# Gate and up of a SwiGLU by seven block products (Strassen) in place of eight, on one core

## The chip, the cores and the metric

The kernel runs on one core of one Trainium2 chip. The metric is device time in microseconds (us), from one launch to its end. The program is one block of straight code and loops for each engine: TensorE (PE), VectorE (DVE), ScalarE (ACT), GpSimd (POOL), and the SyncE queue (SP), which issues every DMA. Engines order each other by semaphores only.

## The reference, cut to what matters

A one-layer encoder over 1024 prompt tokens and 32 sample tokens, all in float32. D_MODEL is 1024, D_FF is 2816.

```python
def swiglu(h, w_gate, w_up, w_down):
    return (jax.nn.silu(h @ w_gate) * (h @ w_up)) @ w_down

def reference(...):
    hp = rms_norm(yp, g_mix)
    q, k, v, u, g = project(hp, w_in)                  # 1792 columns
    a = window_attention_prompt(q, k, v, attn_sinks)
    m = gmlp_prompt(u, g, ...)
    yp = yp + concatenate([a, m]) @ w_out              # 1024 x 1024
    ...                                                # the same for ys
    yp = yp + swiglu(rms_norm(yp, g_ffn), w_gate, w_up, w_down)
    ys = ys + swiglu(rms_norm(ys, g_ffn), w_gate, w_up, w_down)
    y_prompt, y_sample = rms_norm(yp, g_final), rms_norm(ys, g_final)
```

## The kernel before, in words

Tokens are kept as 9 rows: eight tiles of 128 prompt tokens and one of the 32 sample tokens (`SAMPLE`), together `TOK` = 1056 columns. Every large product is made in three passes over fp32r operands (`three_passes`, L611): each operand x is split into a high part (an fp32r copy, by ACT) and a low part (x minus the high part, `low`, by DVE at L1058), and the passes are high*high, high*low and low*high, summed in PSUM. So each 128x128 weight tile of a product costs three pairs of weight load and matmul (L615, L616, L617).

The first part (norm, input projection, attention, gMLP) follows a list written out by hand, `SCHEDULE`. The projection works on 3 token blocks of 352 columns. The output projection follows, row by row (`out_proj`, L797): 48 matmuls of 512 columns for a row of 128 tokens, 32 for the sample row, with w_out in `wbuf`. DVE adds each row's two PSUM banks onto the residual (`add_out_proj`, L1259); ACT squares it, POOL forms the root, DVE scales it (`norm_front`), PE transposes it (`norm_back`, L649), and ACT and DVE write its high and low parts to `t_hl`. The residual of all nine rows stays in on-chip memory (`y_slots`).

The FFN is a loop over 11 chunks of 256 FFN columns (`chunk`, L868). In a chunk PE makes six gate-up steps (`gate_up`, L828: two tiles of 128 FFN columns, three blocks of 352 tokens), each of gate and up with 8 weight tiles and 3 passes, so 48 matmuls of 352 columns. ACT applies Silu, DVE multiplies, and ACT and DVE split the product into `act_hl`. Then PE makes the down product of that chunk for the nine rows (`down`, L850: 12 matmuls of 512 columns for a row of 128 tokens, 8 for the sample row), and DVE adds each row onto the residual (`add_down`, L1311), so the sum over all FFN columns is built up on chip, chunk by chunk. Weights come through a ring of three 4 KB stage slots, and ACT and DVE split them one chunk ahead. After the last chunk the rows are normed and stored.

## Time and profile before

| what | value |
|---|---|
| median of 3 runs | 1141.89 us (1140.77 to 1142.42) |
| profiled execution, its span from first to last instruction | 1140.8 us |
| PE busy | 1109.0 us, 97% of the span |
| PE weight loads busy | 1019.8 us, 89% |
| DVE busy | 482.5 us, 42% |
| ACT busy | 259.4 us, 23% |
| POOL busy | 32.8 us, 3% |
| moved by DMA | 62.71 MB, mean 55 GB/s |
| mean granted TensorE clock | 0.991 |

The span of the profiled execution is the lowest of the three times to 0.1 us, so no time of note lies outside it, and it lies 1.1 us under the median. Durations of matmuls overlap, because they are pipelined: the distance from one start to the next is what a matmul costs, not its length.

### The profile page before, as it was taken

To read this page: it belongs to the slowest core of one execution; us is meant where nothing else is said; L and a number is where in the kernel's file an instruction comes from. 1 tells how busy PE (TensorE), PEld (TensorE's weight loads), DVE (VectorE), ACT (ScalarE), POOL (GpSimd) and SP (SyncE) were. 2 spreads that over 40 slices of the span, in tenths; PEclk is the share of its full clock that TensorE was granted. 3 is DMA by queue.
4 is the path that set the end of the run, shared out by engine and by line. 5 is a ranking of instruction groups with operands and counts; after the bars stand their busy time and mean duration, and the time that the engine had idled before them with its cause. 6 is when DMAs were issued, how large, how long until landed. Compare 5 with 4: busy or idle time off the path is not lost.

```text
span 1140.8 us, 16333 instructions
## 1 busy us (share of the span) xinstructions
PE 1109.0 (97%) x6764; PEld 1019.8 (89%) x6764; DVE 482.5 (42%) x738; ACT 259.4 (23%) x525; POOL 32.8 (3%) x73
## 2 busy tenths in 40 slices
PE   5799999999999999999999999999999999999996
PEld 4799998888888989989899898999989999898995
DVE  4366547655334243342433424243252432524327
ACT  4321245434122211201112021120211211021123
POOL 2101100000000000000000000000000000000002
PEclk9899999999999999999999999999999999999998
DMA  8121332005010131112111021111111201112003
GB/s 279 45 59 39 76 78 57 20 21 189 1 36 3 37 93 31 44 37 55 55 37 53 20 55 55 37 55 37 45 47 37 73 19 55 37 37 74 19 1 153
DMA packets 76120, 62.71 MB, mean 55 GB/s; under 512 B 11888, under 2 KB 68272, under 8 KB 76080
## 3 DMA queue, kind: packets, MB, share of 16 engines
q1 hardware_dynamic: 76080, 62.15, 18.8%
q8 instruction: 29, 0.48, 0.2%
q14 instruction: 11, 0.09, 0.0%
HBM read 57.58 MB, written 4.65 MB: 55 GB/s over the span
## 4 chain that ended last, share of the span: by engine, by line
PE 96%; DVE 2%; ACT 1%; issue 0%; DMA 0%; POOL 0%; POOLq 0%; SPq 0%; ACTq 0%
PE ps L615 30%; PE ps L617 29%; PE ps L616 29%; PE ps L649 1%; PE ps L632 1%; PE ps L633 1%; PE ps L784 1%; DVE work L1078 1%; PE ps L762 1%; PE ps L714 1%; PE ps L746 1%; DMA gain<-in_g_mix 0%; PE ps L703 0%; PE ps L740 0%; ACT work L906 0%
## 5 line engine op out<-in xcount | busy, mean ns | idle before, releaser
L615 PE MATMUL ps<-t_hl,wbuf 128*128 128x352 f32 x864 | 286.1, 331 | 8.4 <-DVE t_hl L1058 8.4
L616 PE MATMUL ps<-t_hl,wbuf 128*128 128x352 f32 x864 | 280.2, 324 | 0.0
L617 PE MATMUL ps<-t_hl,wbuf 128*128 128x352 f32 x864 | 279.9, 324 | 0.0
L1251 DVE TENSOR_TENSOR work<-ps,work 128x1024 f32<-128x1024 f32 (+1 forms) x108 | 132.1, 1223 | 143.0 <-PE ps L617 142.5
L615 PEld LDWEIGHTS ps<-t_hl,wbuf 128*128 128x128 f32 x864 | 164.8, 191 | 10.9 <-DVE t_hl L1058 6.0
L615 PE MATMUL ps<-t_hl,gate_up_a 128*128 128x352 f32 x528 | 170.5, 323 | 0.0
L1298 DVE TENSOR_TENSOR trans<-ps,trans 128x352 f32<-128x352 f32 x66 | 34.6, 524 | 319.2 <-ACT trans L1020 319.2
L616 PE MATMUL ps<-t_hl,gate_up_a 128*128 128x352 f32 x528 | 169.2, 321 | 0.0
L617 PE MATMUL ps<-t_hl,gate_up_a 128*128 128x352 f32 x528 | 169.0, 320 | 0.0
L616 PEld LDWEIGHTS ps<-t_hl,wbuf 128*128 128x128 f32 x864 | 165.2, 191 | 0.0
L617 PEld LDWEIGHTS ps<-t_hl,wbuf 128*128 128x128 f32 x864 | 164.7, 191 | 0.0
L1020 ACT ACTIVATE trans<-ps 128x352 f32<-128x352 f32 x66 | 30.6, 464 | 568.5 <-PE ps L617 568.5
L615 PE MATMUL ps<-wbuf 128*128 128x512 f32 x352 | 138.7, 394 | 0.0
L617 PE MATMUL ps<-wbuf 128*128 128x512 f32 x352 | 138.4, 393 | 0.0
L616 PE MATMUL ps<-wbuf 128*128 128x512 f32 x352 | 137.7, 391 | 0.0
L1058 DVE TENSOR_TENSOR wbuf<-stage,wbuf 128x1024 fp32r<-128x1024 f32 x66 | 80.7, 1223 | 48.1 <-ACT wbuf L925 29.4
L615 PEld LDWEIGHTS ps<-t_hl,gate_up_a 128*128 128x128 f32 x528 | 99.0, 188 | 1.0
L616 PEld LDWEIGHTS ps<-t_hl,gate_up_a 128*128 128x128 f32 x528 | 99.2, 188 | 0.4
L617 PEld LDWEIGHTS ps<-t_hl,gate_up_a 128*128 128x128 f32 x528 | 98.9, 187 | 0.0
L617 PEld LDWEIGHTS ps<-wbuf 128*128 128x128 f32 x352 | 66.1, 188 | 15.4
L616 PEld LDWEIGHTS ps<-wbuf 128*128 128x128 f32 x352 | 66.4, 189 | 14.6
L615 PEld LDWEIGHTS ps<-wbuf 128*128 128x128 f32 x352 | 66.1, 188 | 14.0
(119 smaller groups left out, 997.2 us busy)
## 6 DMA issues: line engine op xcount, KB each, us to landing
stage<-in_w_gate SPq DMA_DIRECT2D x44, 256.0 KB, 3.1
stage<-in_w_up SPq DMA_DIRECT2D x44, 256.0 KB, 3.2
stage<-in_w_down SPq DMA_DIRECT2D x44, 256.0 KB, 3.6
work<-in_x_prompt SPq DMA_DIRECT2D x16, 512.0 KB, 6.5
stage<-in_w_in SPq DMA_DIRECT2D x28, 256.0 KB, 3.5
stage<-in_w_out SPq DMA_DIRECT2D x16, 256.0 KB, 3.8
out_y_prompt<-work SPq DMA_DIRECT2D x8, 512.0 KB, 2.6
gain<-in_g_mix SPq DMA_DIRECT2D x1, 512.0 KB, 5.4
```

The costliest lines, as they stand in the source:

```text
L615: mm(out, wh, xh, start=first, stop=False)
L616: mm(out, wh, xl, start=False, stop=False)
L617: return mm(out, wl, xh, start=False, stop=last)
L632: mm(out, x_both, w_hi, start=first, stop=False)
L633: t = mm(out, x_both, w_lo, start=False, stop=last)
L649: t = turn(out[:, k, 0:n], xn[rows, i % 2, P * k:P * k + P], ident[rows, rows])
L714: t = mm(out[:, P * x:P * x + n], vn[0:n, g % 2, i, :], wsp_t[0:n, g, 0:n], start=True, stop=True)
L746: last = mm(out[DH:P, at:at + P], cat[hp, j, odd:odd + DH], k_t[hp, even:even + P], start=True, stop=True)
L1020: nc.scalar.activation(silu[:, s % 2, :], ps[:, gate_bank(s), 0:BLK], ACT.Silu).then_inc(silu_ready, 1)
L1058: return nc.vector.tensor_tensor(out, x, hi.bitcast(F32), ALU.subtract)
L1251: nc.vector.tensor_tensor(y_row(i), banks(row_parts(i), b), y_row(i), ALU.add).then_inc(added, 1)
L1298: nc.vector.tensor_tensor(hidden[:, s % 2, :], ps[:, gate_bank(s) + 1, 0:BLK], silu[:, s % 2, :], ALU.mult).then_inc(hidden_ready, 1)
```

## The change

Gate and up of one tile of 128 FFN columns are one matrix product of a 2x2 block matrix of weights by a 2x2 block matrix of tokens. The weight blocks are A11 and A12 (gate, first and second half of the 1024 input dimensions) and A21 and A22 (up, likewise). The token blocks are B11 and B21 (rows with even number, first and second half of the dimensions) and B12 and B22 (rows with odd number). Eight block products are replaced by seven (Strassen, in Winograd's form): with sums S1 to S4 of weight blocks and T1 to T4 of token blocks. Each operand form is split in a high and a low part as before, so a block product is 4 tiles by 3 passes, 12 matmuls.

- A step is one tile of 128 FFN columns; there are 22. Each step goes over two halves of the tokens, 256 and 272 columns wide (row pairs 0/1, 2/3; row pairs 4/5, 6/7 and the two halves of the sample row), and makes the seven products in each.
- The seven token forms are made once, row by row, beside the output projection, by copies on ACT and subtractions on DVE. They fill most of on-chip memory. So the residual goes out to device memory (`y_scratch`) row by row after the output projection, and the rows of silu(gate)*up go there too (`hid_scratch`).
- The weight sums are made by four POOL operations of 128x512 in each step; ACT and DVE split all seven weight forms (seven copies and seven subtractions of 128x512).
- ACT copies P1, and P5 and P7 together, out of PSUM; P2, P3 and P4 are summed onto banks in PSUM; DVE makes the remaining sums.
- The down product comes after all 22 steps, with the same 11 chunks of 9 rows and the same matmuls. The chunks' hidden rows and weights are loaded by one DMA each, the residual is loaded back to on-chip memory, and `down` rotates over three pairs of banks in place of two.
- The projection's token blocks are 384, 384 and 288 columns wide, in place of three of 352.

```diff
+PRODUCTS = 7
+P1, P6, P5, P7, P2, P3, P4 = range(PRODUCTS)
+HALF_W = [256, 272]
+BANK_1, BANK_6, BANK_A, BANK_B = [2, 4], [3, 5], [0, 6], [1, 7]
...
             sp.wait_ge(cat_lo, ROWS)
+            load_y(0)
+            load_y(1)
+            for i in range(ROWS):
+                if i == SAMPLE:
+                    sp.wait_ge(wout_unit_done, 1)
+                    load_gate_up(0, 0)
+                    sp.wait_ge(wout_unit_done, 3)
+                    load_gate_up(1, 1)
+                sp.wait_ge(y_added, i + 1)
+                sp.dma_start(y_scratch[row_tokens(i), :], y_row(i)).then_inc(y_spilled[i % 2], 16)
+                if i + 2 < ROWS:
+                    load_y(i + 2)
...
+            def ffn_step(s, q, more):            # SP
+                if more:
+                    sp.wait_ge(w_form_lo, PRODUCTS * s + PRODUCTS)
+                    load_gate_up(s + 2, q)
+                for j in range(2):
+                    store_hidden(s, j)
...
+            last = STEPS - 1
+            sp.wait_ge(product_done, product_count(last, P1, 1))
+            for j in range(2):
+                sp.wait_ge(hidden_out[j], 16 * (STEPS - 2))
+            load_down(0, 0)
+            ffn_step(last - 1, 0, False)
+            sp.wait_ge(w_form_lo, PRODUCTS * STEPS)
+            for i in range(2):
+                sp.wait_ge(y_spilled[i], 16 * len(range(i, ROWS, 2)))
+            for i in range(6):
+                sp.dma_start(y_acc_row(i), y_scratch[row_tokens(i), :]).then_inc(y_back[i], 16)
+            sp.wait_ge(product_done, product_count(last, P3, 1))
+            for i in range(6, ROWS):
+                sp.dma_start(y_acc_row(i), y_scratch[row_tokens(i), :]).then_inc(y_back[i], 16)
+            sp.wait_ge(product_done, product_count(last, P4, 1))
+            load_down(1, 1)
+            ffn_step(last, 1, False)
+            for j in range(2):
+                sp.wait_ge(hidden_out[j], 16 * STEPS)
+            for c in range(2, CHUNKS):
+                load_down(c, c % 2)
...
+            def weight_sums(c, q):               # POOL
+                nc.gpsimd.tensor_tensor(s1, a21, a22, ALU.add).then_inc(w_sum_1, 1)
+                pool.wait_ge(w_sum_1, s + 1)
+                nc.gpsimd.tensor_tensor(s2, s1, a11, ALU.subtract).then_inc(w_sums_ready, 1)
+                nc.gpsimd.tensor_tensor(s3, a11, a21, ALU.subtract).then_inc(w_sums_ready, 1)
+                pool.wait_ge(w_sums_ready, 3 * s + 1)
+                nc.gpsimd.tensor_tensor(s4, a12, s2, ALU.subtract).then_inc(w_sums_ready, 1)
...
+            def product(s, p, j):                # PE
+                elif first and p == P5 and j == 0:
+                    pe.wait_ge(y_added, ROWS)
+                elif not first and p == P1:
+                    pe.wait_ge(c11_silu, 2 * s + (j - 1))
+                elif not first and p == P6:
+                    pe.wait_ge(u2_ready, 2 * s + (j - 1))
+                elif not first and p == P5:
+                    pe.wait_ge(c12_ready, 2 * s + (j - 1))
+                if p == P2:
+                    pe.wait_ge(p1_copied, 2 * s + (j + 1))
+                if p == P3:
+                    pe.wait_ge(p57_copied, 2 * s + (j + 1))
+                if j == 0:
+                    pe.wait_ge(w_form_lo, PRODUCTS * s + (p + 1))
+                for k in range(KH):
+                    w = [wf[:, p, h, k, :] for h in range(2)]
+                    x = [xf[j][:, X_OF[p], h, k, :] for h in range(2)]
+                    t = three_passes(ps[:, bank, 0:HALF_W[j]], w, x, opens and k == 0, k == KH - 1,
+                                     onto=not opens)
...
             for i in range(ROWS):                # ACT, beside the output projection
+                if i >= 1:
+                    plain_forms(i - 1)
+                if i == SAMPLE:
+                    weight_hi(0, 0, 0)
+                norm_front(ROWS + i)
+                if i >= 1:
+                    keep_blocks(i - 1)
...
+            def ffn_step(c, q):                  # ACT
+                copy_p1(s, 0)
+                copy_p57(s, 0)
+                silu_c11(s, 0)
+                silu_c12(s, 0)
+                copy_p1(s, 1)
+                for n in (0, 1, 2):
+                    weight_hi(*following, n)
+                copy_p57(s, 1)
+                weight_hi(*following, 3)
+                silu_c11(s, 1)
+                weight_hi(*following, 4)
+                weight_hi(*following, 5)
+                silu_c12(s, 1)
+                weight_hi(*following, 6)
...
             for i in range(ROWS):                # DVE, beside the output projection
+                if i == SAMPLE:
+                    weight_lo(0, 0, 0)
+                add_out_proj(i)
+                if i >= 1:
+                    if i % 2 == 1:
+                        even_low(i - 1)
+                    else:
+                        odd_blocks(i - 1)
+                if i == SAMPLE:
+                    weight_lo(0, 0, 1)
+                norm_front(ROWS + i)
+                if i >= 2 and i % 2 == 0:
+                    fourth_sum(i // 2 - 1)
+                    if i == SAMPLE:
+                        weight_lo(0, 0, 2)
+                        weight_lo(0, 0, 3)
+                    low_12(i // 2 - 1)
...
+            def blocks(s, j):                    # DVE
+                dve.wait_ge(product_done, product_count(s, P4, j))
+                dve.wait_ge(u2_ready, 2 * s + (j + 1))
+                if not isinstance(s, int) or s >= 1:
+                    dve.wait_ge(hidden_out[j], 16 * s)
...
+            p5_p7(last, 1)                       # DVE, the last step's second half
+            down_weight_lo(0)
+            act_lo(0)
+            blocks(last, 1)
+            hidden(last, 1)
+            for c in range(CHUNKS):
                 for i in range(ROWS):
                     add_down(c, i)
+                    if c + 1 < CHUNKS and i == 1:
+                        down_weight_lo(c + 1)
+                    if c + 1 < CHUNKS and i == 3:
+                        act_lo(c + 1)
```

## Rows read from the trace of the kernel before

**Rows 1.** The page: busy time by engine, and the chain by engine.

```profile
PE 1109.0 (97%) x6764; PEld 1019.8 (89%) x6764; DVE 482.5 (42%) x738; ACT 259.4 (23%) x525; POOL 32.8 (3%) x73
...
PE 96%; DVE 2%; ACT 1%; issue 0%; DMA 0%; POOL 0%; POOLq 0%; SPq 0%; ACTq 0%
```

**Rows 2.** Waits of PE: us in total, times, longest.

```profile
PE ps L649 <- DVE work L1078: 11.9, 4, 8.0
PE ps L615 <- DVE t_hl L1058: 8.4, 3, 4.7
```

**Rows 3.** Stretches of one FFN chunk each: length, busy by engine, clock, DMA.

```profile
371.80:441.50 69.70, 69.70 (x392) 64.86 (x393) 25.93 (x29) 11.51 (x19) 0.00 (x0) 1.00 0.19 53
441.50:511.50 70.00, 70.00 (x396) 65.15 (x395) 25.67 (x28) 11.71 (x19) 0.00 (x0) 1.00 0.17 45
```

**Rows 4.** Timeline of DVE: the sample row's add before and after the FFN.

```profile
362.71 1.22 DVE L1255 TENSOR_TENSOR work<-ps,work 32x1024 f32<-32x1024 f32 x1 [3.00 <-PE ps L633]
...
1132.29 1.22 DVE L1255 TENSOR_TENSOR work<-ps,work 32x1024 f32<-32x1024 f32 x1
```

**Rows 5.** Timeline of PE: first and last of 21 matmuls of 352 columns.

```profile
599.68 0.32 PE L615 MATMUL ps<-t_hl,wbuf 128*128 128x352 f32 x1
...
602.86 0.32 PE L617 MATMUL ps<-t_hl,wbuf 128*128 128x352 f32 x1
```

**Rows 6.** The same, first and last of 18 matmuls of 512 columns.

```profile
429.81 0.39 PE L617 MATMUL ps<-wbuf 128*128 128x512 f32 x1
...
433.72 0.39 PE L633 MATMUL ps<-wbuf 128*64 128x512 f32 x1
```

**Rows 7.** gMLP's mix, plain float32: matmuls and weight loads, merged.

```profile
87.91 1.83 PE L714 MATMUL ps<-wsp_t,work 128*128 128x128 f32 x15
87.92 1.42 PEld L714 LDWEIGHTS ps<-wsp_t,work 128*128 128x128 f32 x12
```

**Rows 8.** Groups of PE, DVE and ACT by shape: busy us, mean ns, idle before.

```profile
L615 PE MATMUL ps<-t_hl,gate_up_a 128*128 128x352 f32 x528 | 170.5, 323 | 0.0
...
L714 PE MATMUL ps<-wsp_t,work 128*128 128x128 f32 x64 | 7.8, 275 | 0.0
...
L1251 DVE TENSOR_TENSOR work<-ps,work 128x1024 f32<-128x1024 f32 x96 | 117.5, 1224 | 142.5 <-PE ps L617 142.5
...
L1058 DVE TENSOR_TENSOR wbuf<-trans,wbuf 128x352 fp32r<-128x352 f32 x66 | 34.7, 525 | 36.5 <-ACT wbuf L1023 36.5
...
L1031 ACT CAST wbuf<-stage 128x1024 fp32r<-128x1024 f32 x44 | 46.0, 1045 | 0.0
...
L1020 ACT ACTIVATE trans<-ps 128x352 f32<-128x352 f32 x66 | 30.6, 464 | 568.5 <-PE ps L617 568.5
```

**Rows 9.** Groups of POOL.

```profile
L575 POOL TENSOR_TENSOR rstd<-meansq,neg_half 128x1 f32<-128x1 f32 x24 | 13.2, 550 | 2.0
...
L587 POOL TENSOR_SCALAR_AFFINE_SELECT work<-work 128x512 f32<-128x512 f32 x1 | 1.7, 1683 | 0.1
```

**Rows 10.** Timeline around the sample row of the output projection.

```profile
354.27 1.04 PE L649 MATMUL ps<-ident,work 128*128 128x128 f32 x8
355.07 0.48 PE L632 MATMUL ps<-wbuf,sample_cat 128*64 128x512 f32 x1
...
362.51 1.03 PE L649 MATMUL ps<-ident,work 128*128 128x128 f32 x8
...
363.30 0.40 PE L615 MATMUL ps<-t_hl,gate_up_a 128*128 128x352 f32 x1
363.58 1.01 ACT L913 CAST t_hl<-ps 128x1024 fp32r<-128x1024 f32 x1 [6.17 <-PE ps L649]
```

**Rows 11.** DMA issues: count, KB each, median us to landing.

```profile
stage<-in_w_gate SPq DMA_DIRECT2D x44, 256.0 KB, 3.1
...
work<-in_x_prompt SPq DMA_DIRECT2D x16, 512.0 KB, 6.5
```

**Rows 12.** Timeline of SP's queue: two column loads issued.

```profile
270.34 0.97 SPq L419 DMA_DIRECT2D stage<-in_w_gate  x2
```

**Rows 13.** Stretches with full DMA queues at the start; columns as in rows 3.

```profile
1.20:8.00 6.80, 0.04 (x1) 0.04 (x1) 1.28 (x1) 2.07 (x4) 1.09 (x5) 1.00 0.85 295
8.00:15.00 7.00, 4.51 (x19) 3.71 (x20) 4.37 (x4) 5.62 (x8) 1.48 (x4) 1.00 1.12 339
```

**Rows 14.** The stretch with PE's starts and stops, early in the span.

```profile
11.00:40.00 29.00, 20.10 (x99) 19.04 (x100) 17.25 (x15) 13.45 (x20) 6.51 (x13) 0.91 0.55 173
```

More of the change, by code:

```diff
@@ new lines, in _, with ffn_step @@
+            for j in range(2):
+                for p in range(PRODUCTS):
+                    product(0, p, j)
+                    if (p, j) == (P2, 0):
+                        norm_back(2 * ROWS - 1)
+            def ffn_step(s):
+                for j in range(2):
+                    for p in range(PRODUCTS):
+                        product(s, p, j)
+            ffn_step(1)
+            with pe.Fori(1, CHUNKS) as c:
+                for q in range(2):
+                    ffn_step(2 * c + q)
@@ L866, in down @@
-                last.then_inc(down_done, 1)
-            def chunk(c, first):
-                for s in range(STEPS):
-                    gate_up(c, s, first)
-                    if first and s == 0:
-                        norm_back(2 * ROWS - 1)
-                for i in range(ROWS):
-                    down(c, i, first)
-            chunk(0, True)
-            with pe.Fori(1, CHUNKS - 1) as c:
-                chunk(c, False)
-            chunk(CHUNKS - 1, False)
+                    x_pair = [act_hl[q][:, h, f, x0:x0 + P] for h in range(2)] if i != SAMPLE else None
@@ L1007, in gather_sample @@
                 if first:
[L1008 removed]
+                    act.wait_ge(wout_unit_done, 4 + n // 2)
                 else:
[L1010 to L1023 removed]
@@ new lines, in _ @@
+            weight_hi(0, 0, 4)
+            copy_p1(0, 0)
+            hi_34(2)
+            hi_34(3)
+            weight_hi(0, 0, 5)
+            weight_hi(0, 0, 6)
+            copy_p57(0, 0)
+            for v in (SAMPLE, SAMPLE + 1):
+                plain_forms(v)
+                keep_blocks(v)
+            silu_c11(0, 0)
+            hi_12(4)
+            hi_34(4)
+            silu_c12(0, 0)
+            copy_p1(0, 1)
+            weight_hi(0, 1, 0)
+            weight_hi(0, 1, 1)
+            weight_hi(0, 1, 2)
@@ new lines, in _ @@
+            last = STEPS - 1
+            copy_p1(last, 0)
+            copy_p57(last, 0)
+            silu_c11(last, 0)
+            silu_c12(last, 0)
+            copy_p1(last, 1)
+            copy_p57(last, 1)
+            down_weight_hi(0)
+            silu_c11(last, 1)
+            act_hi(0)
+            silu_c12(last, 1)
+            for c in range(CHUNKS):
+                gather_sample(c)
+                if c + 1 < CHUNKS:
+                    down_weight_hi(c + 1)
+                    act_hi(c + 1)
@@ new lines, in _ @@
+            weight_lo(0, 0, 4)
+            second_u(0, 0)
+            low_34(2)
+            low_34(3)
+            weight_lo(0, 0, 5)
+            weight_lo(0, 0, 6)
+            p5_p7(0, 0)
+            even_low(SAMPLE)
+            odd_blocks(SAMPLE + 1)
+            fourth_sum(4)
+            low_12(4)
+            low_34(4)
+            blocks(0, 0)
+            hidden(0, 0)
+            second_u(0, 1)
+            weight_lo(0, 1, 0)
+            weight_lo(0, 1, 1)
+            weight_lo(0, 1, 2)
@@ L1311, in add_down @@
             def add_down(c, i):
                 dve.wait_ge(down_done, ROWS * c + (i + 1))
+                if c == 0:
+                    dve.wait_ge(y_back[i], 16)
+                b = DOWN_BANKS[i % 3]
                 if i == SAMPLE:
[L1314 to L1325 removed]
+                    sample_low(b, y_acc_row(i), c + 2)
@@ L1326, in chunk @@
+                add_banks(i, b, y_acc_row(i), y_acc)
+            last = STEPS - 1
+            second_u(last, 0)
+            p5_p7(last, 0)
+            blocks(last, 0)
+            hidden(last, 0)
+            second_u(last, 1)
+            p5_p7(last, 1)
[3 more added lines that the diff above has]
+            hidden(last, 1)
+            for c in range(CHUNKS):
                 for i in range(ROWS):
                     add_down(c, i)
-                    if not last and i in (0, 2):
-                        split_chunk(c, 4 + i // 2)
```

696 lines of the change are left out of this document (482 added, 214 removed).

## The prediction

> **What bounds the kernel now.** First the busy times and the chain: PE is busy 97% of the span and the chain lies on it for 96% [rows 1]. So time is won only by giving PE less to do, and lost wherever PE waits. PE's list of waits is short: some 20 us, all before the FFN [rows 2]. Next the stretches: an FFN chunk takes 70 us, PE is busy in all of it at the full clock, while DVE is busy 26 us and ACT 12 [rows 3]. The sample row's add is seen at 362.71 us and, eleven chunks later, at 1132.29 [rows 4]: 769.6/11 = 69.96 us for a chunk. That is 67% of the span, and the place of the change.
>
> What a matmul costs is the distance of starts. 352 columns: (602.86-599.68)/20 = 0.159 us [rows 5]. 512 columns: (433.72-429.81)/17 = 0.230 [rows 6]. Down is 104 matmuls a chunk, 23.9 us; what is left for the 288 of gate-up is 46.0 us, 0.1599 each, which agrees with [rows 5]. At 2.4 GHz the columns alone are 0.1467 and 0.2133: 13 ns and 17 ns on top. Weight loads are hidden under the matmuls.
>
> **What goes and what comes on PE.** Gone: 11 x 46.0 = 506 us of gate-up. New: 22 steps x 7 products x 12 matmuls x 2 halves = 3696 matmuls of 256 and 272 columns (before: 3168 of 352). Columns fall by an eighth, matmuls rise by a sixth, so all hangs on the cost of a short one, which this trace does not show. Bounds: the line through 352 and 512 columns (slope 0.000438) gives 0.118 and 0.125, mean 0.1215; the columns plus all of the 13 ns give 0.1197 and 0.1263, mean 0.123. From below: gMLP's plain float32 matmuls of 128 columns are recorded with 275 ns, against 323 for 352 fp32r columns, so they stream for about as long as 256 columns; their starts lie (1.83-0.275)/14 = 0.111 us apart, and their full weight loads, recorded with 0.19 us, (1.42-0.19)/11 = 0.112 [rows 7, 8]. So a load and a stream of 0.107 us do overlap: 0.111 and 0.118, mean 0.1145. I take 0.119, between the two. 3696 x 0.119 = 440 us: **66 us gained**. Ends: 0.1145 gives 423 (83 gained); from above only the 352-column matmul itself bounds it, 0.1599, 591 us (85 lost). I take the value near the row it is nearest to, and for the range allow 0.127, 469 us (37 gained), since load and stream of equal length may disturb each other.
>
> By the row, a full load is hidden under a stream as long as 256 columns [rows 7], so the sum takes it as hidden. The Trainium skill (TensorE: Matmul & The Clock Gate, LDWEIGHTS) puts a load at columns over 1.2 GHz, 107 ns for 128, with no fast load for fp32: exactly the length of a 256-column stream, so a narrower half would gain nothing. Its gap for a lone matmul, N/2.4 + 2.5 ns, would make 112.5 ns on average, 416 us and a gain of 90, 24 more than my sum; the 13 and 17 ns above speak against that here.
>
> The down product moves but keeps its matmuls: 11 x 23.9 = 263 us. The projection's blocks of 384, 384, 288 have the columns of before: nothing.
>
> **Other engines in a step** (PE 20.0 us). Lengths from 352 and 1024 columns [rows 8]: DVE 0.165 + 1.04 per 1000, ACT 0.18 + 0.83. DVE: 7 x 0.70 for the low parts, 4 x 0.71 for the wide sums, 6 x 0.44 for the others, 10.4 at most. ACT: 7 x 0.61 + 4 x 0.40 + 2 x 0.40 + 2 x 0.62 = 7.9 us. POOL: four 128x512; nearest is a select of that size, 1.68 us, and a one-column operation at 0.55 [rows 9]: 2.2 to 6.7 us. All lie under PE. A weight form is written after its product in the second half and wanted six products later, 8.5 us; its chain (sums, ACT 0.61, DVE 0.70, what is queued ahead) is under 4. One wait is tight: P3 reuses the banks of P5 and P7. P7's record ends some 0.17 us after its stream, the copy takes 0.62, P2 covers 1.4; a half microsecond is left, and the next load wants 0.2. I charge 1.5 us for the run; if the cover fails, 0.5 us x 44 = 22.
>
> The row here shows no DVE and POOL operation hindering each other. The Trainium skill (SBUF — State Buffer, the shared port pair) says a DVE operation with two SBUF inputs and a POOL operation reading SBUF exclude each other: in a step DVE would then wait up to POOL's 6.7 us and still end within 20, and only the start below would pay, about 1.5 us. I leave it out of the sum.
>
> **Output projection.** Per row pair (PE 23 us) DVE has about 12 us and ACT 8, hidden. The residual is loaded two rows ahead, after the split of cat; 512 KB lands in 6.5 us when many are queued [rows 11]; the first may come 2 to 4 us late, which the second bank pair covers (11 us).
>
> **Start of the FFN.** Before, the first gate-up matmul follows the transposes at 363.3 without a wait [rows 10]. Now the weights of step 0 overwrite w_out: SP may issue only after the first unit of the sample row (355.07 + 0.93 + 0.2), four DMAs at 0.5 each, 3.1 to land [rows 10 to 12]: 361.5. But ACT first writes row 7's form after the transposes (363.6 + 0.6), then weight form 0, then DVE's low part: P1 starts at 365.7. From here DVE's queue is the line, since its first weight form now stands ahead of the sample row's adds. Behind it come the two adds of the sample row (to 368.0); ACT squares that row and keeps row 7's half (to 369.9); then four DVE operations on row 7 (to 372.8) and low part 1: P6 at 373.6. The norm of the sample row (1.3), fourth sum, low parts 2, 3, the pair of T1 and T2 (1.23), 4, u, two pairs of T3 and T4 (2.5), 5 and 6 follow: the last at 383, P4 ends at 385.2. Without waits seven products of 1.43 and the sample's transposes would end at 374. **11 us**, and 1 us more before the second half (small forms of the sample row): 12. Ends 8 and 17.
>
> **From gate-up to down.** T is the end of P1 in the last step's second half. Only then SP issues load_down(0,0), 2.1 MB, and behind it in the same queue the store of step 20. DVE's blocks(21,0) waits for that store, ACT's silu_c12(21,0) for it, and in ACT's queue behind that stands copy_p1(21,1), for which PE's P2 waits. Full queues move 295 to 339 GB/s [rows 13]: 2.4 MB is 7.5 us, plus 2.5 of issue and landing, T+10; P2 starts at T+12 in place of T+4.4, P4 ends at T+16.7. The down weights' high and low parts (2.0 and 2.3) and the hidden rows' (2.0 and 2.4), in line behind it, end at T+19.2. PE would have been free at T+9: **10 us**, with ends 5 (if the store overtakes) and 15. Then 4.3 MB of residual are loaded ahead of load_down(1,1), which DVE wants in place of an add at row 1: 8 MB in all at 0.32 is T+28, some 5 us after it is wanted; three bank pairs cover most, 1 us, up to 6.
>
> Waits as long as these cost clock: between 11 and 40 us, where PE stands still for 9 us in pieces, it is at 0.91, so some 5 us at 1.2 GHz [rows 14]. I charge 2.5 us for both places, up to 5.
>
> The tail after the last down row is the same.
>
> **Sum.** -66 + 12 + 10 + 1 + 1.5 + 2.5 = -39, on the span of 1140.8; the median of the runs is 1.1 above it, so on the median 1141.9 - 39, rounded, is **1103 us**.
>
> **Rivals.**
> - A, the forecast: short matmuls near 0.119, waits only at the two joints. Alone 1088 to 1120. Chance 0.58.
> - B, waits in each half step (the P5/P7 copy comes too late, or a queue behind it): 0.5 to 0.7 us x 44 = 22 to 31 us more, 1125 to 1134. For it: half a microsecond of slack. Against: ACT is 60% idle. 0.15.
> - C, the short matmul costs only its stream (0.1145) and the joints are as counted: 17 less, 1086 or lower. For it [rows 7], against it the 13 ns of [rows 5]. 0.12.
> - D, slower: load and stream of 0.107 us no longer overlap cleanly. It decides at (506-27)/3696 = 0.1296 us; at 0.135 the gate-up costs 499 and the time is 1142 - 7 + 27 = 1162. For it: never were both this close with fp32r. Against: [rows 7]. 0.10.
> - E, joints far dearer (30 to 40 us more, from DMA order or a late store): 1133 to 1143. 0.05.
>
> A measurement here tells 0.2%, 2.3 us. Slower needs D beyond 0.130 or E at its end: 0.09. Same: 0.03. Faster: 0.88. The range takes A, most of B and part of C: 1083 to 1130.
>
> **What the profile would show.** Starts of the L-lines of three_passes 0.115 to 0.122 us apart in a step of 20 us; 22 steps, 440 us; DVE 10 and ACT 8 us busy in each. PE idle before P1 and P6 of step 0, released by DVE; idle before P2 of the last step, released by ACT, with the DMA of hid_scratch ahead in the chain; down chunks of 24 us. Wrong, if starts lie over 0.125 apart, or PE's waits for the copy of P5 and P7 sum to more than 5 us.

## The result and the profile after

The changed kernel takes 1116.66 us (median of 4 runs), 1142.14 for the one before beside it: ratio 0.977, 95% interval 0.9754 to 0.9786. Timed again beside later experiments it took 1116.95 us, ratio 0.9774 (0.9761 to 0.9788). Times are medians, and ratios leave out one execution of 2100 us (one of six with the weights first), whose cause is open. So it is faster by 25.5 us, where 39 were forecast; 1116.66 lies in the range, on its upper side.

The page of the changed kernel, answering to [rows 1]: busy times, and the chain by engine.

```profile
PE 1065.8 (96%) x7292; PEld 975.6 (88%) x7292; DVE 663.3 (59%) x967; ACT 351.6 (32%) x711; POOL 165.2 (15%) x161
...
PE 90%; DVE 5%; DMA 2%; ACT 1%; issue 1%; POOL 1%; SPq 0%; POOLq 0%; ACTq 0%; DVEq 0%
```

PE is still the bound, but 10% of the chain now lies elsewhere, where it was 4%. Where that is, stretches of the changed kernel tell (columns as in [rows 3]): the start of the FFN, one step of seven products, the joint from gate-up to down, one down chunk.

```profile
360.00:386.00 26.00, 16.31 (x103) 15.46 (x102) 21.32 (x31) 12.98 (x25) 11.87 (x10) 0.74 0.33 92
438.63:459.30 20.67, 20.67 (x170) 20.67 (x169) 12.04 (x18) 7.40 (x15) 6.10 (x4) 1.00 0.26 78
820.00:842.00 22.00, 14.24 (x96) 13.72 (x95) 8.05 (x9) 5.58 (x7) 0.00 (x0) 0.84 0.83 308
842.00:866.00 24.00, 24.00 (x105) 19.13 (x104) 15.35 (x12) 5.04 (x8) 0.00 (x0) 1.00 0.81 299
```

In a step PE is busy from end to end at the full clock, and the records of the weight loads now touch too (20.67 of 20.67; before, 65 of 70 us [rows 3]). At the two joints PE is busy 16 of 26 and 14 of 22 us, and the clock is at 0.74 and 0.84.

The first matmul of each half of that step, on PE's timeline, answers to [rows 5]:

```profile
438.63 0.28 PE L768 MATMUL ps<-x_forms,w_forms 128*128 128x256 f32 x1
...
448.70 0.29 PE L768 MATMUL ps<-x_forms,w_forms 128*128 128x272 f32 x1
...
459.30 0.28 PE L768 MATMUL ps<-x_forms,w_forms 128*128 128x256 f32 x1
```

84 matmuls of 256 columns in 10.07 us are 0.1199 us each, 84 of 272 in 10.60 are 0.1262. The mean is 0.1231, and 3696 of them take 455 us, not 440.

PE's waits from 355 us on, answering to [rows 2]: us in total, times, longest.

```profile
PE ps L768 <- DVE w_forms L1402: 7.4, 2, 4.3
PE ps L768 <- ACT ffn_u L1262: 6.2, 1, 6.2
PE ps L768 <- DVE x_forms L1402: 2.3, 1, 2.3
PE ps L768 <- DVE act_even L1402: 1.6, 1, 1.6
```

Five waits, 17.5 us in all: the first and third line at the start, the others at the joint to down, none in the steps between.

**The account on the spans** (1140.8 to 1114.8, 26.0 less). The last transposes ahead of the FFN end at 360.4, not 363.5: -3.1. Gate-up took 505 us (what is left after 263 for down between 363.5 and 1131.5, one distance behind the last matmul's start), and takes 22 x 20.67 = 455: -50. From the transposes' end to the first matmul of step 1 (397.28) there are 36.9 us, one step and 16.2 more; from the last step's P1 (810.75) to down's first matmul (841.25) 30.5, one step and 9.8 more: together +26. Down takes 264.3: +1.3. The tail is the same. Sum: -26.

### The profile page after: what moved, and what is told of

It reads as the page before. It is cut to its first block, busy times and chain, and to the rows that moved or that the text cites. A ratio compares the mean times of both kernels' runs of the same rounds, so it can differ in the third digit from the quotient of the medians.

```text
span 1114.8 us, 18490 instructions
## 1 busy us (share of the span) xinstructions
PE 1065.8 (96%) x7292; PEld 975.6 (88%) x7292; DVE 663.3 (59%) x967; ACT 351.6 (32%) x711; POOL 165.2 (15%) x161
## 4 chain that ended last, share of the span: by engine, by line
PE 90%; DVE 5%; DMA 2%; ACT 1%; issue 1%; POOL 1%; SPq 0%; POOLq 0%; ACTq 0%; DVEq 0%
PE ps L768 28%; PE ps L769 27%; PE ps L770 27%; PE ps L805 1%; PE ps L782 1%; PE ps L783 1%; PE ps L940 1%; PE ps L918 1%; DMA hid_scratch<-ffn_blocks 1%; DMA out_state_gmlp_v_sample<-work 1%; DVE work L1422 1%; PE ps L902 1%; DVE work L1487 1%; DVE ln_st L1481 0%; DVE work L1498 0%
## 5 line engine op out<-in xcount | busy, mean ns | idle before, releaser
L768 PE MATMUL ps<-x_forms,w_forms 128*128 128x256 f32 (+1 forms) x1232 | 355.6, 289 | 15.9 <-DVE w_forms L1402 7.4
L769 PE MATMUL ps<-x_forms,w_forms 128*128 128x256 f32 (+1 forms) x1232 | 356.1, 289 | 0.0
L770 PE MATMUL ps<-x_forms,w_forms 128*128 128x256 f32 (+1 forms) x1232 | 355.0, 288 | 0.0
L768 PEld LDWEIGHTS ps<-x_forms,w_forms 128*128 128x128 f32 x1232 | 237.7, 193 | 16.8 <-ACT ffn_u L1262 6.4
L770 PEld LDWEIGHTS ps<-x_forms,w_forms 128*128 128x128 f32 x1232 | 237.3, 193 | 0.0
L769 PEld LDWEIGHTS ps<-x_forms,w_forms 128*128 128x128 f32 x1232 | 237.2, 193 | 0.0
L1595 DVE TENSOR_TENSOR y_low<-ps,y_low 128x1024 f32<-128x1024 f32 x66 | 80.7, 1223 | 41.0 <-PE ps L770 41.0
L768 PE MATMUL ps<-w_dn_even,act_even 128*128 128x512 f32 x192 | 75.8, 395 | 1.6 <-DVE act_even L1402 1.6
L770 PE MATMUL ps<-w_dn_even,act_even 128*128 128x512 f32 x192 | 75.5, 393 | 0.0
L769 PE MATMUL ps<-w_dn_even,act_even 128*128 128x512 f32 x192 | 75.2, 392 | 0.0
L1402 DVE TENSOR_TENSOR w_forms<-w_sums,w_forms 128x512 fp32r<-128x512 f32 x88 | 60.7, 690 | 22.6 <-ACT w_forms L1254 21.0
L1254 ACT CAST w_forms<-w_sums 128x512 fp32r<-128x512 f32 x88 | 54.5, 621 | 45.9 <-PE ps L770 45.9
L768 PE MATMUL ps<-w_dn_odd,act_odd 128*128 128x512 f32 x160 | 63.2, 395 | 0.0
L770 PE MATMUL ps<-w_dn_odd,act_odd 128*128 128x512 f32 x160 | 62.9, 393 | 0.0
L769 PE MATMUL ps<-w_dn_odd,act_odd 128*128 128x512 f32 x160 | 62.7, 392 | 0.0
L1595 DVE TENSOR_TENSOR y_high<-ps,y_high 128x1024 f32<-128x1024 f32 (+1 forms) x33 | 40.3, 1221 | 32.2 <-PE ps L770 31.8
L1740 DVE TENSOR_TENSOR ffn_blocks<-ffn_blocks 128x512 f32<-128x512 f32 (+1 forms) x44 | 52.9, 1203 | 4.8 <-ACT ffn_blocks L1286 4.8
L768 PEld LDWEIGHTS ps<-w_dn_even,act_even 128*128 128x128 f32 x192 | 36.1, 188 | 10.0 <-issue 1.8
```

The lines of the kernel that those rows point to most:

```text
L768: mm(out, wh, xh, start=first, stop=False, skip_group_check=onto)
L769: mm(out, wh, xl, start=False, stop=False, skip_group_check=onto)
L770: return mm(out, wl, xh, start=False, stop=last, skip_group_check=onto)
L1254: nc.scalar.copy(wf[:, n, 0, :, :], src).then_inc(w_form_hi, 1)
L1402: return nc.vector.tensor_tensor(out, x, hi.bitcast(F32), ALU.subtract)
L1595: nc.vector.tensor_tensor(y, banks(row_parts(i), b), y, ALU.add).then_inc(added, 1)
```

## Experiments

Three kernels were timed in a single execution and have no ratio; the others have one with its 95% interval. The medians of the kernel before, timed beside them, lie between 1141.2 and 1142.6 us.

**What a short matmul costs: fewer tokens.** All products take 192 and 208 token columns in place of 256 and 272.

```diff
-                    x = [xf[j][:, X_OF[p], h, k, :] for h in range(2)]
-                    t = three_passes(ps[:, bank, 0:HALF_W[j]], w, x, opens and k == 0, k == KH - 1,
+                    x = [xf[j][:, X_OF[p], h, k, 0:[192, 208][j]] for h in range(2)]
+                    t = three_passes(ps[:, bank, 0:[192, 208][j]], w, x, opens and k == 0, k == KH - 1,
```

> The kernel after the change with the block products over 192 and 208 columns in place of 256 and 272 (the last 64 columns of each half are left out, so the outputs are not the reference's). It tells what a short matmul costs. Theory (columns at 2.4 GHz plus 13 ns, as the change shows for 256, 272, 352): starts lie 0.093 and 0.100 us apart. Rival (the floor is the weight load, 0.107 us and its 13 ns): they stay at 0.120 or only fall to 0.107 to 0.112, the spacing of gMLP's weight loads before. A third way: fp32r streams slower under 256 columns: 0.2 us or more.

One execution: 1072.72 us. First matmuls of the halves on PE's timeline of this kernel:

```profile
420.76 0.28 PE L768 MATMUL ps<-x_forms,w_forms 128*128 128x208 f32 x1
...
430.14 0.27 PE L768 MATMUL ps<-x_forms,w_forms 128*128 128x192 f32 x1
...
439.52 0.28 PE L768 MATMUL ps<-x_forms,w_forms 128*128 128x208 f32 x1
```

Both halves take 9.38 us: 0.1117 us a matmul for 192 and for 208 columns. So something else than the stream sets the pace there, as the rival has it.

**The same with half the weight columns.** Token columns of 256 and 272, weight columns 64 in place of 128.

```diff
-                    w = [wf[:, p, h, k, :] for h in range(2)]
+                    w = [wf[:, p, h, k, 0:64] for h in range(2)]
...
-                    t = three_passes(ps[:, bank, 0:HALF_W[j]], w, x, opens and k == 0, k == KH - 1,
+                    t = three_passes(ps[0:64, bank, 0:HALF_W[j]], w, x, opens and k == 0, k == KH - 1,
```

> The kernel after the change with weight tiles of 64 columns in place of 128 in the block products: half of the FFN columns are left out and their PSUM rows hold old values, so the outputs are not the reference's. Matmuls keep 256 and 272 token columns. A load of 64 weight columns should take half the time. Theory (the 13 ns over the columns are a fixed cost of a matmul, not of a load as long as the stream): starts stay at 0.120 and 0.126. Rival (load and stream of equal length get in each other's way): they fall to 0.109 to 0.112 for 256 columns.

One execution: 1099.9 us. A half of 272 columns begins at 423.67, one of 256 at 434.16, the next at 443.69: 0.1249 and 0.1135 us each. That is neither of the two expectations: the 256 columns fell by 6.4 of the 8 to 11 ns that the rival has, the 272 by 1.3.

**Both at once.** 192 and 208 token columns, 64 weight columns (the two edits above together).

> The kernel after the change with block products of 192 and 208 token columns and weight tiles of 64 columns (a quarter of the columns of both kinds is left out or more, so the outputs are not the reference's). With 192 and 208 columns and full tiles every matmul cost 0.1117 us, whatever its columns. Theory: that floor is the load of 128 weight columns; with 64 it goes, and starts lie 0.087 to 0.093 us apart for 192 and 0.094 to 0.100 for 208. Rival: the floor is not the load (the issue of a pair, a read of the tokens): it stays at 0.11.

One execution: 1008.84 us. Its halves on PE's timeline:

```profile
418.47 0.26 PE L768 MATMUL ps<-x_forms,w_forms 128*64 128x208 f32 x1
...
426.59 0.25 PE L768 MATMUL ps<-x_forms,w_forms 128*64 128x192 f32 x1
...
434.04 0.26 PE L768 MATMUL ps<-x_forms,w_forms 128*64 128x208 f32 x1
```

0.0967 and 0.0887 us, as expected. The floor of 0.1117 is gone with half the weight columns. The record of a load falls with them from 190 to 135 ns, so the load is the likely floor; but a tile of 64 weight columns also gives half the rows of output, and no run parts the two. Together (us from start to start; "columns" is the stream at 2.4 GHz):

| token columns | columns alone | 128 weight columns | 64 weight columns |
|---|---|---|---|
| 192 | 0.0800 | 0.1117 | 0.0887 |
| 208 | 0.0867 | 0.1117 | 0.0967 |
| 256 | 0.1067 | 0.1199 | 0.1135 |
| 272 | 0.1133 | 0.1262 | 0.1249 |

With half the load the short streams cost 7 to 12 ns on top. At 256 columns the full load costs 6.4 ns more than the half one, at 272 still 1.3. That fits a load and a stream of nearly equal length disturbing each other, by 6.4 ns where they are nearest; how they do it no run shows. Rival D decides at 0.1296 us, another 9.7 ns above the 0.1199.

The Trainium skill (TensorE: Matmul & The Clock Gate, LDWEIGHTS) puts a load at its columns over 1.2 GHz, 107 ns for 128; the floor seen here lies 5 ns above that. The gap that the same page of the Trainium skill (Back-to-back issue gap) gives for a lone matmul, N/2.4 + 2.5 ns, is not reached by any cell of the table: the least is 7 ns above the stream.

**Narrow blocks without Strassen.** The kernel before, its gate-up in four blocks of 264 tokens in place of three of 352: 4224 matmuls, classical products.

```diff
+FB = 4
+FBLK = TOK // FB
-STEPS = 2 * BLOCKS
+STEPS = 2 * FB
...
-                        last = three_passes(ps[:, gate_bank(s) + g, 0:BLK], w,
+                        last = three_passes(ps[:, gate_bank(s) + g, 0:FBLK], w,
```

> The kernel before, with its gate-up in four token blocks of 264 columns in place of three of 352: eight products, but short matmuls, 4224 of them in place of 3168. It parts the change in two: narrower blocks, and one product in eight saved. Theory (columns plus 13 ns): 0.1233 us each, 521 us in place of 505: 16 us more, 1158; so Strassen at equal width saves 65 us, and the width takes back 13 to 16 of it. Rival (0.1145 by the gMLP rows, as for load and stream of 0.107): 0.114 to 0.118 each, 482 to 498: 7 to 23 less.

1152.58 us against 1141.18, ratio 1.009 (1.0075 to 1.0104), between the two expectations and nearer to the first. Two chunks' adds of the sample row on its DVE timeline:

```profile
506.23 1.22 DVE L1257 TENSOR_TENSOR work<-ps,work 32x1024 f32<-32x1024 f32 x1 [0.61 <-PE ps L635]
...
576.87 1.22 DVE L1257 TENSOR_TENSOR work<-ps,work 32x1024 f32<-32x1024 f32 x1 [0.61 <-PE ps L635]
```

A chunk takes 70.64 us, 23.9 of it down: 46.7/384 = 0.1217 us a matmul, 514 us for gate-up where 352 columns took 505. So narrowness costs 9 us, and seven products in place of eight at about that width take 514 to 455, 59 us. (The other 2 to 3 us of the 11.4 lie outside the steady chunks; the first chunk there takes 72.3.)

**Blocks of 384, 384, 288 alone.** The kernel before, with the projection's blocks of the change and nothing else of it.

```diff
+PB_W = [384, 384, 288]
...
-                cols = slice(BLK * b, BLK * b + BLK)
+                cols = slice(384 * b, 384 * b + PB_W[b])
...
-                    last = three_passes(ps[:, proj_bank(n), 0:BLK], w, (t_hi[:, k, cols], t_lo[:, k, cols]),
+                    last = three_passes(ps[:, proj_bank(n), 0:PB_W[b]], w, (t_hi[:, k, cols], t_lo[:, k, cols]),
```

> The kernel before, with one part of the change alone: the projection's token blocks are 384, 384 and 288 columns wide in place of three of 352, and the split of cat waits by these blocks. In the trace after, the transposes ahead of the FFN end 3.1 us earlier than in the trace before, 2.0 of it by the first output projection matmul and 1.1 over its rows. Theory: the blocks bring the 2.0 (row 2 needs one block less, and there are fewer waits at the end of the projection), and the 1.1 belongs to where the token forms lie: 1140, 2 us less, with rows of the output projection still 12.0 us apart. Rival: the blocks bring nothing and the 2 us come from elsewhere: 1142.

1139.48 us against 1141.18, ratio 0.9988 (0.9979 to 0.9996): 1.7 us less, which the sum had at nothing. The output projection's rows are as far apart as before (11.98 us), where the changed kernel has the first six 11.8 apart: 1.1 us over all rows. It is in both profiles of the change and isn't the blocks'; that it is the other layout of the token forms is argued, not shown. With the 1.7 it makes most of the 3.1 us ahead of the FFN.

**GpSimd's share.** The weight sums of steps 2 on are formed by DVE, not by GpSimd.

```diff
-            with pool.Fori(1, CHUNKS) as c:
-                for q in range(2):
-                    weight_sums(c, q)
...
+                dve.wait_ge(w_landed[q], 64 * c + 64)
+                dve.wait_ge(w_form_lo, PRODUCTS * s - PRODUCTS + (W_S4 + 1))
+                nc.vector.tensor_tensor(s1, a21, a22, ALU.add).then_inc(w_sum_1, 1)
...
                 p5_p7(s, 0)
+                weight_sums(*following)
                 blocks(s, 0)
```

> The kernel after the change, with the weight sums of steps 2 to 21 made by DVE (four operations of 128x512 in each step, ahead of the block sums of the first half) in place of POOL. In the trace after, DVE's operations with two on-chip operands take 1.5 to 1.8 us in place of 0.7 while POOL makes the sums. Theory: DVE and POOL exclude each other there, and it costs nothing because PE is the line: DVE's operations are all back at 0.69 to 0.72, DVE's busy time in a step stays near 13 us (10.4 and 2.8), a step stays at 20.67 us, and the time is that of the change to 1 us. Rival 1: the exclusion delays something PE waits for: a step gets shorter, by up to 0.5 us, 10 us in all. Rival 2: the long operations have another cause (a wait for an operand inside them): they stay long with POOL idle.

1115.52 us, ratio 0.9776 (0.9764 to 0.9789): no change, as expected. But see one operation of `hidden`, both its inputs on chip, first in the changed kernel (groups of DVE, 420 to 800 us; busy, mean ns):

```profile
L1740 DVE TENSOR_TENSOR ffn_blocks<-ffn_blocks 128x544 f32<-128x544 f32 x19 | 34.5, 1814 | 0.0
```

and then with GpSimd idle:

```profile
L1737 DVE TENSOR_TENSOR ffn_blocks<-ffn_blocks 128x544 f32<-128x544 f32 x19 | 13.6, 718 | 0.0
```

and a step of that kernel:

```profile
437.00:457.70 20.70, 20.70 (x170) 20.70 (x169) 12.26 (x22) 7.41 (x15) 0.00 (x0) 1.00 0.26 78
```

1814 ns against 718: the operation sits out most of one of GpSimd's, which take 1.3 us or more. DVE is busy 12.26 us a step with four more operations of 0.69, so 9.5 without them, and 2.5 of the 12.04 in the changed kernel were such waiting. None of it reaches PE. The Trainium skill (SBUF — State Buffer, Who interferes with whom) says that a DVE instruction with two SBUF inputs and a GpSimd instruction that reads SBUF contend, and that one blocks until the other is done; the 1814 and 718 ns agree.

**The store ahead of the loads.** SP issues the store of the step before the last ahead of the first down load, not behind it.

```diff
             last = STEPS - 1
+            ffn_step(last - 1, 0, False)
 
             sp.wait_ge(product_done, product_count(last, P1, 1))
             for j in range(2):
                 sp.wait_ge(hidden_out[j], 16 * (STEPS - 2))
             load_down(0, 0)
-            ffn_step(last - 1, 0, False)
```

> The kernel after the change, with one move in SP's queue: the two stores of step 20's hidden rows are issued before the wait for P1 of the last half step, not behind the 2.1 MB of down loads. Theory: the stall of PE before P2 of the last half step (6.5 us in the trace after) hangs on the store alone, through blocks(21,0), the Silu behind it and copy_p1(21,1) in ACT's queue. Then that stall is gone, PE stays at the full clock there, and the first down row starts when the down loads and their high and low parts are done, about 12 us after the end of P1 in place of 18.8: 7 to 8.5 us less than the change, 1108 to 1110. Rival: the down loads and their parts are the line and the store stands beside it: the stall at P2 goes, the first down row still starts at 18.8, and the time falls by under 1 us.

1108.15 us, ratio 0.9729 (0.9707 to 0.975): 8.5 us less than the change by the medians. The median flatters it: the five times are 1107.3, 1107.5, 1108.2, 1113.3 and 1113.5, and the ratios, 0.9729 against 0.977 and 0.9774, are only 5 us apart. The joint in the changed kernel, from the timeline of all engines:

```profile
822.53 0.39 SPq L641 DMA_DIRECT2D w_down_even<-in_w_down  x1
822.97 0.46 SPq L644 DMA_DIRECT2D hid_even<-hid_scratch  x1
823.49 1.23 SPq L621 DMA_DIRECT2D hid_scratch<-ffn_blocks  x2
...
831.76 0.69 DVE L1728 TENSOR_TENSOR ffn_blocks<-ps,ffn_u 128x512 f32<-128x512 f32 x1 [14.02 <-DMA hid_scratch<-ffn_blocks]
...
832.49 0.42 ACT L1286 ACTIVATE ffn_blocks<-ffn_blocks 128x256 f32<-128x256 f32 x1 [13.96 <-DVE ffn_blocks L1728]
832.81 0.37 ACT L1262 COPY ffn_u<-ps 128x272 f32<-128x272 f32 x1
...
833.23 0.59 PE L768 MATMUL ps<-x_forms,w_forms 128*128 128x272 f32 x1 [6.19 <-ACT ffn_u L1262]
...
841.25 0.47 PE L768 MATMUL ps<-w_dn_even,act_even 128*128 128x512 f32 x1 [1.56 <-DVE act_even L1402]
```

and with the store first:

```profile
817.09 0.69 DVE L1728 TENSOR_TENSOR ffn_blocks<-ps,ffn_u 128x512 f32<-128x512 f32 x1 [3.28 <-PE ps L770]
...
818.60 0.39 SPq L641 DMA_DIRECT2D w_down_even<-in_w_down  x1
...
823.65 1.91 ACT L1362 CAST w_dn_even<-w_down_even 128x2048 fp32r<-128x2048 f32 x1
...
826.03 1.96 ACT L1367 CAST act_even<-hid_even 128x2112 fp32r<-128x2112 f32 x1 [0.17 <-DMA hid_even<-hid_scratch]
...
828.02 2.36 DVE L1402 TENSOR_TENSOR act_even<-hid_even,act_even 128x2112 fp32r<-128x2112 f32 x1
...
830.64 0.47 PE L768 MATMUL ps<-w_dn_even,act_even 128*128 128x512 f32 x1 [2.99 <-DVE act_even L1402]
```

In the changed kernel the chain reads upwards from 833.23: PE's P2 waits for ACT's copy, which stands behind the silu, which waits for DVE's blocks, which waits 14 us, nearly 11 of them for a store that SP issued behind 2.1 MB of loads. With the store first DVE waits for PE alone, 3.3 us. From the second half's P1 to the first down matmul there are 816.89 to 830.64, 13.75 us, against 20.42: 6.7 less. The stall at P2 is gone and down starts 12.2 us after the end of P1, as expected. Of the 6.7 this execution gives 1.6 back: the first 24 us of down ran at a granted clock of 0.93, where the changed kernel has 1.00, and so has the kernel with both orders below. The rest of the 8.5 the edit can't have made: the transposes ahead of the FFN end anywhere between 358.3 and 362.1 us in the profiles of kernels that are alike up to there. What is left is the line of the splits of down weights and hidden rows; PE still waits 3.0 us for its end.

**Weights first at the start.** On ACT and DVE the splits of step 0's weights stand ahead of the work on the tokens of the last rows. Shown is ACT's queue; DVE's is changed in the same way.

```diff
                 if i == SAMPLE:
                     weight_hi(0, 0, 0)
+                    weight_hi(0, 0, 1)
+                    weight_hi(0, 0, 2)
                 norm_front(ROWS + i)
+                if i == SAMPLE:
+                    weight_hi(0, 0, 3)
+                    weight_hi(0, 0, 4)
+                    copy_p1(0, 0)
...
+                    weight_hi(0, 0, 5)
+                    weight_hi(0, 0, 6)
...
-            weight_hi(0, 0, 4)
-            copy_p1(0, 0)
             hi_34(2)
             hi_34(3)
-            weight_hi(0, 0, 5)
-            weight_hi(0, 0, 6)
             copy_p57(0, 0)
```

> The kernel after the change, with another order at the start of the FFN alone: on ACT and DVE all seven weight forms of step 0 come ahead of the operations on row 7's and the sample row's token forms, which only the second half needs. Theory: DVE's queue is the line from the first weight form to the second half of step 0 (some 19 us of work for it), so the stall before P6 (4.7 us) goes but comes back before P1 of the second half: the time falls by 1 to 4 us only. Rival: what costs is the stall before P6 and the half clock after it (4.7 and 4 to 5 us): all of it goes, 8 to 10 us less.

1114.76 us, ratio 0.9765 (0.9751 to 0.9778): 2 us less, with an interval that overlaps that of the change. The waits for weight forms fall from 7.4 to 3.4 us, and a new one stands in their place (waits of PE in this kernel):

```profile
PE ps L768 <- ACT ffn_q L1273: 6.5, 1, 6.5
```

The copy of P5 and P7, for which P3 waits, now stands in ACT's queue behind the token sums' splits, and these wait for DVE. So the time came out as the first expectation has it, but the stall came back before P3 and not before the second half.

**Both orders.** The last two edits together.

> The kernel after the change with both: the store of step 20 first, and the weight forms of step 0 first. Theory: the two places are 440 us apart and have nothing in common, so the gains add: 8 to 12 us less than the change, 1105 to 1109. Rival: they do not add, because the clock or a DMA ties them.

1107.82 us, ratio 0.9711 (0.9696 to 0.9726), on the same chip as the 1108.15 and 1114.76 above: 8.8 us less than the change by the medians, 7 by the ratios. From the second half's P1 to down there are 13.7 us, as with the store alone. Nearly all of it is the store, and the gains of the two places add within the scatter.

**Down weights early.** From both orders: the down weights, which need no stored row, are loaded from the first half's P1 on, and split ahead of the last P5/P7 work.

```diff
+            sp.wait_ge(product_done, product_count(last, P1, 0))
+            sp.dma_start(w_down_in[0][:, :, :], w_down[:, 0:2, :]).then_inc(w_down_landed[0], 16)
             sp.wait_ge(product_done, product_count(last, P1, 1))
...
-            copy_p57(last, 1)
             down_weight_hi(0)
-            silu_c11(last, 1)
+            copy_p57(last, 1)
             act_hi(0)
+            silu_c11(last, 1)
...
-            p5_p7(last, 1)
             down_weight_lo(0)
+            p5_p7(last, 1)
```

> The kernel of both moves, and further: the first down weights are loaded when P1 of the last step's first half is done (the place that they overwrite is read by nothing later), and their high and low parts are made ahead of the copy of P5 and P7; only the hidden rows are left to load and split behind the last half step. In the trace with the store first, the first down row starts 12.0 us after the end of P1, and PE is free after 8.9. Theory: what is left of that wait is the chain of two loads and four operations on ACT and DVE, one after the other; with the weights' part moved out of it the chain ends at 10: 2 to 3.5 us less than both moves together, about 1105. Rival: the wait hangs on the hidden rows' load, behind other loads in the queue: under 1 us less.

1104.39 us, ratio 0.9671 (0.9657 to 0.9685): 3.4 us less than both orders, as expected. From the second half's P1 to down 820.12 to 831.50, 11.4 us (13.75 with the store alone), of which 10.6 are the half itself.

**The change once more**, beside the last kernels.

> The kernel after the change once more, unchanged, on the chip of the others, so that the small gains of the reordered kernels are read against it. Both theories: 1114 to 1117, ratio 0.976 to 0.978; in the trace the same two places of waiting, 15 to 17 and 9.5 to 10 us over the step time, and the start of the output projection between 256 and 258.5 us.

1116.95 us; over the step time its joint at the start is 15.0 us, and from P1 of the second half to down there are 20.3 us, 9.7 over the half. The output projection starts at 259.8 us, outside the 256 to 258.5 expected.

**ACT's copy forward, GpSimd's sums back.** From the kernel with early down weights.

```diff
                     weight_hi(0, 0, 5)
                     weight_hi(0, 0, 6)
+                    copy_p57(0, 0)
...
             hi_34(3)
-            copy_p57(0, 0)
...
+            pool.wait_ge(t_34_lo, 5)
             weight_sums(0, 1)
```

> From the run that joins both orders and starts the down weights early (1104.4 us, 1142.6 for the kernel before beside it) two things are changed at the start of the gate-up phase, nothing else: ScalarE's copy of P5 and P7 of the first half stands right behind the splits of the first weights, in front of the splits of the token sums; and GpSimd holds the weight sums of step 1 back until all low parts of the token sums have been formed. Theory 1, the order on ScalarE and the sharing between GpSimd and VectorE set the start: the wait of 6.5 us before P3 of the first half goes, VectorE's chain there is some 2.6 us shorter (its operations of 512 columns at 0.69 us and not 1.7), and the second half starts 2 to 3 us earlier against the end of the sample's transposes; part of what the P3 wait was comes back ahead of the second half. 1.5 to 3 us less than 1104.4, that is 1101.5 to 1103, ratio 0.965. Theory 2, VectorE's own amount of work between the transposes and the second half (19.7 us of 24.6 busy) is the line: less than 1 us, the wait only moves from P3 to the P1 of the second half, 1103.5 to 1104.5. Theory 3, the weight sums of step 1 now come late: a wait at the second product of step 1 or later there, and the time is 1 us or more above 1104.4.

1104.16 us, ratio 0.9671 (0.9657 to 0.9685): nothing (theory 2 of the three). Stretches of this kernel, the two halves of step 0:

```profile
360.60:380.85 20.25, 14.14 (x92) 13.24 (x93) 16.82 (x28) 11.41 (x22) 4.81 (x6) 0.77 0.31 89
380.85:393.44 12.59, 12.59 (x85) 12.59 (x85) 7.70 (x11) 5.22 (x10) 5.37 (x4) 0.83 0.06 22
```

and of the kernel that it came from:

```profile
364.09:385.99 21.90, 15.10 (x92) 14.37 (x93) 19.45 (x27) 10.65 (x21) 9.83 (x8) 0.77 0.26 79
385.99:396.58 10.59, 10.59 (x86) 10.59 (x85) 6.48 (x11) 5.22 (x10) 0.00 (x0) 1.00 0.08 26
```

DVE's busy time fell by 2.6 us, as reckoned, and the first half is shorter by 1.7. But the wait of 6.5 us before P3 became one of 5.3 us before the second half, and the 1.2 GHz that follows a wait of that length now falls on the second half, 12.59 us in place of 10.59. The two halves together are 0.35 us longer; from the transposes' end to step 1 there are 34.9 us, against 35.5.

## Why the prediction was right in sign and 13.5 us short

**The step that failed is the cost of the short matmul.** The working took 0.119 us "between the two" and got 440 us; measured are 0.1231 and 455, a gain of 50 and not 66. Its own upper bound, the columns plus all of the 13 ns, gave 0.1197, 0.1263 and 0.123, and that is what came, to the nanosecond. What drew the value down was the bound from below, 0.1145 by [rows 7]: float32 matmuls whose starts lie 0.111 us apart were read as "load and stream of 0.107 us do overlap". The narrow runs show what those rows can tell: with 128 weight columns nothing starts closer than 0.1117 us, even with 192 token columns. So they bound the load and say nothing of the few ns that a 256-column stream costs on top. Of the 13 ns at 256 columns 6.4 go with the second half of the weight columns, the rest is there with 64 of them too; the row to trust was the one of the same kind, [rows 5]. One part is open: 264 columns in the kernel before cost 0.1217, while 0.1231 is the mean about that width here; which part of the layout or the traffic costs that 1.4 ns (5 us in all) wasn't tried.

**The joints: the sum right, the parts not.** +12, +10 and 2.5 for the clock are 24.5; measured are 16.2 and 9.8, 26.0. At the start PE waits 9.7 us and its busy time is 27.2 us for what would take some 21.6 at the full clock (a step, and about one us for the sample's transposes): the low clock costs some 5.5 there, and at the end 2.1 (20.4 us from P1 of the second half to down, less 7.8 of waits, for a half of 10.6), so 7.6 and not 2.5, and the waits by themselves were over-counted. At the start the reorderings did little. From the transposes' end to step 1 the four profiled kernels with the change's own order there (the change twice, the store first, the sums on DVE) take 36.9, 35.6, 35.1 and 37.7 us, the four with another order 35.0, 34.8, 35.5 and 34.9: some 1.3 less in the mean, within the scatter of the first four. Each wait that was taken away came back at the next place, and the low clock behind it. The 16.2 us too are one profile's; in the others it is 14.4 to 17.1, so that the sum of the joints met its forecast this closely is in part luck. That DVE's queue is the line there fits these runs; it is not shown, since no run took work from DVE there, only its waiting for GpSimd. At the end the mechanism was as written, store behind the load, DVE, ACT's queue, P2, and P2 and down's start came out nearly as timed: P2 was forecast at 12 us after the end of P1 and came at 10.9, down at 19.2 and came at 18.9. The runs with the store first and with early down weights show it by taking 6.7 and then 2.4 us of it away.

**What was costed at nothing.** The projection's blocks are worth -1.7 us (measured by themselves; 0.5 to 2.4 by the interval), the output projection's rows another -1.1, read in the trace; in the second profile of the change only 1.4 of the 3.1 us are there. The copy of P5 and P7, 1.5 us, costs nothing in any of the 21 later steps. Down: +1 forecast, +1.3 measured. The exclusion between DVE and GpSimd was named at 1.5 us for the start and left out; it lengthens four DVE operations there by some 3.8 us, and taking most of it away moved nothing.

So on the spans: -50 for -66 (16 missed), -3.1 for nothing, 26 for 24.5, 0 for 1.5, 1.3 for 1; together -26 for -39.

**Rivals.** B, waits in each half step: none in the list of waits. C, the bare stream: no full load with 256 or 272 token columns reaches the 0.1145. D: what goes with the full load is 6.4 ns at 256 columns, already inside the 0.1231, and D decides at 0.1296. E: the joints came as counted. A is what happened, at the dear end of its short matmul; "alone 1088 to 1120" holds 1116.7.

## What to carry to other kernels

Cost a narrower matmul as its columns plus the surcharge seen on matmuls of the same kind and the nearest width, and use a row of another kind only for what bounds that row. A product saved by Strassen is worth its share of PE's time, less the surcharge on every matmul that the narrower blocks add, less what PE waits at the joints between phases. The order in a queue can decide that: here one move, a store ahead of a load on the same queue, took 6.7 us out of a joint, a quarter of what the whole change had won. At the start of the FFN a wait that was removed came back one step later, so time such a joint from end to end before and after, not the wait. And take more than one profile: this joint scattered by 2.6 us between kernels that are alike there, more than the reorderings gained.

## What the runs showed of the hardware

- A floor of 0.1117 us from start to start for fp32r pairs of load and matmul with 128 weight columns, the same at 192 and at 208 token columns; with 64 weight columns 0.0887 and 0.0967.
- The surcharge over the columns is not one figure: 13 ns at 256 and 272 columns with a full load, 7 and 12 with half of it, 17 at 512 [rows 6]. And it is there at the full clock alone. In the changed kernel, behind the stall at P2, twelve distances of 272 columns take 2.72 us:

```profile
834.08 0.43 PE L768 MATMUL ps<-x_forms,w_forms 128*128 128x272 f32 x1
...
836.80 0.37 PE L768 MATMUL ps<-x_forms,w_forms 128*128 128x272 f32 x1
```

  That is 0.2267 us each, 272 columns at 1.2 GHz and nothing on top, where 0.1262 is the distance at 2.4 GHz. So a matmul at the low clock costs 1.8 times, not twice, as much.
- A DVE operation of 544 columns with both inputs on chip takes 1.81 us beside GpSimd's sums and 0.72 without, while the ratios of the whole kernel, 0.977 and 0.9776, don't differ.
- After a wait of 5.3 us PE's matmuls go on at 1.2 GHz for a while (granted clock 0.83 over the half that follows): that half costs 2.0 us more.
